# Latent attention projected feature-wise, its softmax weights and two other branches' scaled on ScalarE, and the first weight group converted in halves

## The reference, cut to what matters

```
u = rms_norm(h, norm_pre);  proj = u @ w_in
A: q  = rms_norm(c_q) @ w_uq        (192 -> 4 heads x (64 plain + 32 rotary))
   kv = rms_norm(c_kv) @ w_ukv      (128 -> 4 heads x (64 key + 64 value))
   rotary(q[64:96]), rotary(k_rope) shared by the heads; causal softmax(q k) v
B: dilated window attention;  C: top-128 keys of an indexer;  D: two softmax maps, p0 - lambda p1
y = concat(each branch * silu(gate)) @ w_out;  h = h + rms_norm(y, norm_post)
```

## Time and profile before

| | |
|---|---|
| median of three runs | 771.83 us (767.22 to 775.15) |
| the profiled execution | 768.9 us, its span 767.0 us |
| PE busy | 690.5 us, 90% of the span |
| DVE busy | 450.4 us, 59% |
| ACT busy | 328.7 us, 43% |
| POOL busy | 218.4 us, 28% |
| mean granted clock | 0.954 of full |

### The profile page before, as it was taken

The page is one execution under the profiler, slowest core; times in us unless marked ns, Lnnn a source line. Parts: engine busy times, 40 slices in busy tenths (PEclk is TensorE's granted clock), DMA queues, the critical chain, the costliest instruction groups (busy, mean ns, idle before and its releaser), DMA issues. The chain is left out here.

```text
span 767.0 us, 10353 instructions
## 1 busy us (share of the span) xinstructions
PE 690.5 (90%) x3836; PEld 553.9 (72%) x3836; DVE 450.4 (59%) x1067; ACT 328.7 (43%) x750; POOL 218.4 (28%) x91
## 2 busy tenths in 40 slices
PE   3996999998989899889998999999898989988996
PEld 2885877787776674448997887788787767444896
DVE  4211597987688645561182158888978864556214
ACT  4422534654223445571434345456432344457221
POOL 1332241424035430200335342324323543020020
PEclk9998999997899976999999999999999997699999
DMA  8457963423122110202353487542322221020112
GB/s 259 123 188 233 258 185 111 124 76 106 55 69 69 69 56 1 109 1 80 96 157 111 129 254 228 157 138 69 98 70 68 70 70 56 0 108 3 43 42 110
DMA packets 66753, 81.47 MB, mean 106 GB/s; under 512 B 10720, under 2 KB 52320, under 8 KB 66703
## 3 DMA queue, kind: packets, MB, share of 16 engines
q1 hardware_dynamic: 66703, 80.81, 34.2%
HBM read 70.28 MB, written 13.93 MB: 110 GB/s over the span
## 5 line engine op out<-in xcount | busy, mean ns | idle before, releaser
L694 POOL TENSOR_TENSOR w_low<-w_raw,w_high 128x2048 fp32r<-128x2048 f32 (+2 forms) x39 | 175.8, 4507 | 435.3 <-ACT w_high L733 435.3
L1215 PE MATMUL bank<-uT,w_high 128*128 128x512 f32 x400 | 161.2, 403 | 0.0
L1217 PE MATMUL bank<-uT,w_low 128*128 128x512 f32 x400 | 159.2, 398 | 0.0
L1216 PE MATMUL bank<-uT,w_high 128*128 128x512 f32 x400 | 159.1, 398 | 0.0
L837 ACT ACTIVATE probs<-probs,negmax 128x128 f32<-128x128 f32 (+3 forms) x160 | 89.1, 560 | 99.6 <-DVE negmax L1070 99.0
L1215 PEld LDWEIGHTS bank<-uT,w_high 128*128 128x128 f32 x400 | 76.2, 190 | 18.7 <-issue 1.9
L1217 PEld LDWEIGHTS bank<-uT,w_low 128*128 128x128 f32 x400 | 76.2, 190 | 18.0
L1216 PEld LDWEIGHTS bank<-uT,w_high 128*128 128x128 f32 x400 | 76.3, 191 | 16.5
L733 ACT ACTIVATE w_high<-w_raw 128x2048 fp32r<-128x2048 f32 (+2 forms) x40 | 74.7, 1868 | 29.8 <-DMA w_raw<-in_w_out 23.7
L1215 PE MATMUL bank<-w_high,mix 128*128 128x256 f32 x256 | 72.4, 283 | 1.0 <-DVE mix L1155 1.0
L1216 PE MATMUL bank<-w_low,mix 128*128 128x256 f32 x256 | 71.6, 280 | 0.0
(11 more groups left out here) (145 smaller groups left out, 1119.0 us busy)
## 6 DMA issues: line engine op xcount, KB each, us to landing
w_raw<-in_w_in SPq DMA_DIRECT2D x28, 1024.0 KB, 5.4
w_raw<-in_w_out SPq DMA_DIRECT2D x8, 1024.0 KB, 4.9
parts_dram<-staging SPq DMA_DIRECT2D x12, 512.0 KB, 5.9
strips<-strips_dram SPq DMA_DIRECT2D x24, 256.0 KB, 4.6
dqk<-parts_dram SPq DMA_DIRECT2D x24, 256.0 KB, 4.3
hX<-in_x SPq DMA_DIRECT2D x8, 512.0 KB, 5.8
strips_dram<-table_dram SPq DMA_DIRECT2D x1, 3328.0 KB
qidx<-parts_dram SPq DMA_DIRECT2D x12, 256.0 KB, 4.2
```

The costliest lines, as they stand in the source:

```text
L694: nc.gpsimd.tensor_tensor(w_low[:, s, :, 0:w], w_raw[:, s, :, 0:w], w_high[:, s, :, 0:w].bitcast(F32), ALU.subtract).then_inc(w_low_done, 1)
L1215: nc.tensor.matmul(out_ap, lh, rh, start=start, stop=False)
L1216: nc.tensor.matmul(out_ap, lh, rl, start=False, stop=False)
L1217: return nc.tensor.matmul(out_ap, ll, rh, start=False, stop=stop)
```

## The change

1. The order of the start is by token block: u0, cv0, u1, cv1, u2, cv2, u3, cv3, in both layers. In layer 0 group 0 is asked for before the second block of x, in two halves of its rows, and rounded (ACT) and reduced (DVE) in halves by a new step `first_low` behind u0. cv0 starts with the first half.
2. `norm` of the jobs of B, C and A: DVE takes only the reciprocal, ACT multiplies (four activations a job, 24 jobs in the two layers). D stays.
3. Branch A is projected feature-wise. `aq h`: one head's queries for all tokens, [128 x 512] in two products; the weight's columns are loaded so that rows 64 to 95 hold the rotary features and 96 to 127 the same with their halves swapped. ACT copies rows 0 to 63, and DVE multiplies rows 64 to 127 by cos and by -sin, sin (`trig`). The scores then contract over 128 rows. The query's root is not applied to q, but as a factor in the scores' L1070 (`negroot`). `aroot` spreads the key's root over the partitions by four products and DVE multiplies `latkv` by it; `ak`, `av` give keys (two heads each) and values.
4. The shared rotary key is made on POOL in three operations at `norm 8`, with two more loads, and copied by two transfers to the eight row groups of `aqk` at `norm 9`. `wuq` and `wukv` come in eight loads instead of three.

```diff
-HEAD_UNITS = [("u", 0), ("u", 1), ("unit", "cv", 0), ("u", 2), ("unit", "cv", 1), ("unit", "cv", 2), ("u", 3),
+HEAD_UNITS = [("u", 0), ("unit", "cv", 0), ("u", 1), ("unit", "cv", 1), ("u", 2), ("unit", "cv", 2), ("u", 3),
               ("unit", "cv", 3)]
...
+FIRST_START = [("hmean", 0), ("hnorm", 0), HEAD_UNITS[0], ("first_low",), ("hmean", 1), ("hnorm", 1), HEAD_UNITS[1],
+               HEAD_UNITS[2], ("hmean", 2), ("hnorm", 2), HEAD_UNITS[3], HEAD_UNITS[4], ("hmean", 3), ("hnorm", 3),
+               HEAD_UNITS[5], HEAD_UNITS[6], HEAD_UNITS[7]]
...
-    [HEAD_UNITS[1], 3, ("hmean", 3), HEAD_UNITS[2], HEAD_UNITS[3], ("hnorm", 3), HEAD_UNITS[4], HEAD_UNITS[5],
+    [HEAD_UNITS[1], HEAD_UNITS[2], 3, ("hmean", 3), HEAD_UNITS[3], HEAD_UNITS[4], ("hnorm", 3), HEAD_UNITS[5],
      HEAD_UNITS[6], HEAD_UNITS[7]]
...
-             10: [("aup", 0), ("aup", 1), ("aturn", 0)],
-             11: [("aup", 2), ("aturn", 1), ("aup", 3), ("aturn", 2), ("aturn", 3)]}
+             10: [("aq", 0), ("aq", 1), ("aroot",), ("aq", 2)],
+             11: [("aq", 3), ("ak", 0), ("ak", 1), ("av", 0), ("av", 1)]}
...
+                if step == ("norm", 8):
...
+                    nc.gpsimd.tensor_tensor(raw, raw, trig[HD:A_QK, :], ALU.mult).then_inc(kr_step, 1)
+                    pool.wait_ge(kr_step, 2 * l + 1)
+                    nc.gpsimd.tensor_tensor(turn, turn, trig2[HD:A_QK, :], ALU.mult).then_inc(kr_step, 1)
+                    pool.wait_ge(kr_step, 2 * (l + 1))
+                    nc.gpsimd.tensor_tensor(raw, raw, turn, ALU.add).then_inc(kr_ready, 1)
...
+                if kind == "first_low":
+                    w = WIDTH[0]
+                    for half in range(2):
+                        ks = slice(half * KC // 2, (half + 1) * KC // 2)
+                        act.wait_ge(first_loaded[half], 16 * len(GROUPS[0][1]))
+                        nc.scalar.activation(w_high[:, 0, ks, 0:w], w_raw[:, 0, ks, 0:w], ACT.Copy
+                                             ).then_inc(w_high_done if half else first_high, 1)
...
+                if kind == "norm" and MAPS[step[1]] == 1:
+                    j = step[1]
+                    buf = probs[probs_buffers(j)[0]]
+                    act.wait_ge(inv_ready, scaled(l, j))
+                    for q in range(NB):
+                        pr = buf[:, POFF[q]:POFF[q] + WID[q]]
+                        ins = nc.scalar.activation(pr, pr, ACT.Copy, scale=inv[:, j % 4, 0, q:q + 1])
+                    ins.then_inc(probs_scaled, 1)
...
+                if kind == "ak":
+                    n = l * NU + UNIT_AT[step]
+                    act.wait_ge(unit_ready, n + 1)
+                    for half in range(2):
+                        ins = nc.scalar.activation(aqk[0:HD, 1, 2 * step[1] + half, :],
+                                                   bank[HD * half:HD * (half + 1), unit_bank(n), :], ACT.Copy)
+                    ins.then_inc(emptied_by["act"], 1)
...
-                    after(nc.vector.reciprocal(inv[:, i, 0], sums[:, i, 0]))
-                    for q in range(NB):
-                        sl = slice(POFF[q], POFF[q] + WID[q])
-                        ins = nc.vector.tensor_scalar(probs[bufs[0]][:, sl], probs[bufs[0]][:, sl],
-                                                      inv[:, i, 0, q:q + 1], None, ALU.mult)
-                ins.then_inc(probs_ready, 1)
+                    nc.vector.reciprocal(inv[:, i, 0], sums[:, i, 0]).then_inc(inv_ready, 1)
...
+                if kind == "aq":
...
+                    dve.wait_ge(high_written, highs(n))
+                    nc.vector.tensor_tensor(aqk[HD:P, 0, step[1], :], bank[HD:P, unit_bank(n), :], trig[HD:P, :],
+                                            ALU.mult).then_inc(emptied_by["dve"], 1)
...
+                if kind == "aq":
+                    h = step[1]
+                    pe.wait_ge(a_folded, l + 1)
+                    b = work_bank(l * NU + UNIT_AT[step])
+                    nc.tensor.matmul(b, wuq[:, 0, h, :], latq[:, 0, :], start=True, stop=False)
+                    nc.tensor.matmul(b, wuq[0:QL - P, 1, h, :], latq[0:QL - P, 1, :], start=False, stop=True
+                                     ).then_inc(unit_ready, 1)
+                if kind == "aroot":
...
+                    for tb in range(NB):
+                        ins = nc.tensor.matmul(b[:, tb * P:(tb + 1) * P],
+                                               roots[:, r, NB + tb:NB + tb + 1].to_broadcast([P, P]), ident[:],
+                                               start=True, stop=True)
+                    ins.then_inc(unit_ready, 1)
+                if kind == "ak":
+                    wait_unit_emptied(pe, l * NU + UNIT_AT[("aroot",)])
+                    b = work_bank(l * NU + UNIT_AT[step])
+                    nc.tensor.matmul(b, wukv[:, 0, step[1] * P:(step[1] + 1) * P], latkv[:], start=True, stop=True
+                                     ).then_inc(unit_ready, 1)
```

More of the change, by code:

```diff
@@ L74 @@
 SEL_BLOCKS = (3, 2, 1)
-N_CONSTS = 12
+N_CONSTS = 10
 TOPK_ROUNDS = 3 * TOPK // 8
@@ L241, in units_of @@
         return ["dve"]
[L242 to L247, removed]
+    if k in ("aup_head", "aq", "aroot"):
+        return ["dve"]
+    if k in ("ak", "av"):
+        return ["act"]
     return []
@@ L338, in convert_steps @@
         for s in STEPS[freed + 1:]:
-            cost += {"unit": 1 if s[0] == "unit" and GROUPS[GI[s[1]]][2] else 2, "aup": 1, "pv": 1}.get(s[0], 0)
+            cost += {"unit": 1 if s[0] == "unit" and GROUPS[GI[s[1]]][2] else 2, "aq": 1, "ak": 1, "pv": 1}.get(s[0], 0)
             if cost >= CONVERT_AFTER.get(g, 4):
@@ L877, in _ @@
-                if kind == "aturn":
-                    tb = step[1]
-                    n = l * NU + UNIT_AT[step]
-                    for i in range(2):
-                        act.wait_ge(unit_ready, n + 1 + i)
-                        nc.scalar.activation(aqk[0:A_QK, i, :, tb * P:(tb + 1) * P],
-                                             bank[0:A_QK, unit_bank(n + i), :].rearrange(
-                                                 "p (h t) -> p h t", h=HEADS),
-                                             ACT.Copy).then_inc(emptied_by["act"], 1)
+                    act.wait_ge(unit_ready, n + 1)
@@ new lines, in _ @@
+                    nc.scalar.activation(aqk[0:HD, 0, step[1], :], bank[0:HD, unit_bank(n), :], ACT.Copy
+                                         ).then_inc(high_written, 1)
+                if kind == "ak":
+                    n = l * NU + UNIT_AT[step]
+                    act.wait_ge(unit_ready, n + 1)
+                    for half in range(2):
+                        ins = nc.scalar.activation(aqk[0:HD, 1, 2 * step[1] + half, :],
+                                                   bank[HD * half:HD * (half + 1), unit_bank(n), :], ACT.Copy)
+                    ins.then_inc(emptied_by["act"], 1)
@@ L886, in _ @@
+                if kind == "av":
+                    i = step[1]
+                    n = l * NU + UNIT_AT[step]
+                    if i == 0:
+                        act.wait_ge(pv_ready, l * NPV + PV_OF[7] + 1)
+                    act.wait_ge(unit_ready, n + 1)
+                    nc.scalar.activation(values[0][:, 2 * i:2 * i + 2, :].rearrange("p t c -> p (t c)"),
+                                         bank[:, unit_bank(n), :], ACT.Copy).then_inc(emptied_by["act"], 1)
                 if kind == "mix":
@@ L1399, in _ @@
+                if kind == "av":
+                    b = work_bank(l * NU + UNIT_AT[step])
+                    for half in range(2):
+                        tb = 2 * step[1] + half
+                        ins = nc.tensor.matmul(b[:, half * 256:(half + 1) * 256], latkv[:, tb * P:(tb + 1) * P],
+                                               wukv[:, 1, :], start=True, stop=True)
+                    ins.then_inc(unit_ready, 1)
                 if kind == "ya":
```

217 lines of the change are left out of this document (107 added, 110 removed).

## The result

The changed kernel takes 797.95 us (median of four runs, 793.57 to 805.73). The kernel before takes 772.5 on the same chip. The ratio is 1.0319 [1.0221, 1.0417]: slower, by about 25 us, where I had said 781 and a range up to 794. The direction was right, the size was not. The profiled executions differ by more than the medians, 799.7 against 767.0 us of span.

A forecast was written before the change was run, and what follows sets the result against it. PE, busy for 90% of the span, was taken as the bound. Terms 4.2 + 5.8 + 3.4 + 3.4 - 5.6 + 6.0 - 5.8 = +11.4 on 768.9 gave 780.3, stated as 781, range 766 to 794.

The forecast's parts named there:

- Clocks are set even: Whole kernel: half-clock time unchanged, what `turn 7` gets back against what new waits lose; nothing in the sum.
- The projections of A: From `aup_head` to the first A score, 40.0 before: feature-wise projections save 2.9 a layer, -5.8 in all.
- ScalarE's normalisation: ACT's multiplications delay awaited copies: +3.4 at bv, +3.4 at `pv 4`, -5.6 at `turn 7`, +6.0 in A's jobs.
- The jobs of A: Branch A's four jobs: ACT's multiplications don't fit beside its other work without delay, +3.0 a layer.
- The starts: Layer starts: cv units wait behind their own u and group 1's conversion, +4.2 in layer 0, +5.8 in layer 1.
- Further falls of the clock: Rival: new stretches without products at cv2 and bv lower the clock; three falls give 790, range 785 to 796, chance 0.20.
- The rival in which `turn 7` keeps the clock: 6.8 at half clock there goes, -3.4 a layer; with cheaper starts 767, one of both 774; shared chance 0.20.
- hiding ScalarE's work wholly: Rival: ACT's normalisation delays only where ACT was waited for; wholly hidden, 9 less, 772; chance 0.08.

The follow-up runs named there:

- e3: Feature-wise projections alone, in the kernel before (multiplications on DVE, old start): ratio 0.9911 [0.9851, 0.9971].
- e4: The changed kernel with the multiplications back on DVE, new start and projections kept: ratio 0.9998 [0.9932, 1.0064] to the kernel before.
- e9: e3 with job 7's weights multiplied by ScalarE, all else as in the kernel before: ratio 0.9899 [0.9834, 0.9964] to the kernel before.
- e1: ScalarE's multiplications alone, in the kernel before (old start, old projections): ratio 1.0223 [1.009, 1.0355].
- e5: The changed kernel with the old start, keeping ScalarE's multiplications and feature-wise projections: ratio 1.0286 [1.0231, 1.0342] to the kernel before.
- e12: The changed kernel with the dense products of e10 among the sums of squares: four executions, 801.16, 804.61, 798.17 and 776.41, too far apart for a ratio.
- e10: e9 with three dense products, results unread, among the sums of each token block: ratio 0.9847 [0.9749, 0.9945] to the kernel before.
- e6: The changed kernel with additional products, results unused, in PE's waits at cv2 of layer 0, bv2, `pv 4`, `pv 6`: ratio 1.0298 [1.0229, 1.0368] to the kernel before.
- e2: The new start alone (order by token block in both layers, group 0 early in halves), in the kernel before: ratio 1.0103 [0.998, 1.0227].
- e8: e3 with branch A's sums of squares one job slot earlier and job 7 multiplied by ScalarE: ratio 0.9931 [0.9886, 0.9975] to the kernel before.
- e7: The kernel before with branch A's sums of squares at the end of job slot 8 instead of 9: ratio 1.0381 [1.0301, 1.0461].

## Why the prediction was wrong

**The step that failed: the clock.** The sum has it in one sentence: "Clocks are set even: what `turn 7` gets back against what new waits lose." In the projections it keeps the stretch at half clock for a constant 17, as both layers of before showed it, and in branch A's jobs it has none. The traces, by stage, both layers together; the last column is the measured change less the forecast in the table above:

| stages | us at 1.2 GHz before | after | over the forecast |
|---|---|---|---|
| the two starts | 0 | 10.2 | +1.7 |
| cq to bv2 | 20.5 | 21.7 | -1.0 |
| bv2 to sums | 13.6 | 15.8 | +2.4 |
| sums to first A score | 34.2 | 51.2 | +10.9 |
| from the first A score on | 0 | 13.6 | +6.8 |
| sum | 68.3 | 112.5 | +20.8 |

The 44.2 us more at half clock are at most 22.1 of the 32.2 by which the two executions differ. The rest, 10.1 or more, stands against my 11.4: the waits were sized nearly right, and the clock, put at nothing, is the miss.

**The projections of A.** Forecast -5.8, in the changed kernel +5.1. The feature-wise code has 6.8 us at half clock or 24 to 27 (20.5 with the wait at `pv 6` filled), with stages of 31.9 or 41 (e3, e4). The long form comes with VectorE's multiplications too (four of six layers in e3, e4 and e9), so it isn't ScalarE's. In the changed kernel both layers were long: 27.3 and 23.9, that is 10.2 and 6.8 more than before, at most 8.5 of time. ACT's longer chain (4.5 for `pv 6` instead of 3.2) and the fold's 1.33 are the rest. That e3's ratio agrees with the -5.8 is luck in part: it rests on four of ten executions, and in e3's trace one layer gained 8.1 and the other lost 0.9.

**ScalarE's normalisation.** +7.2 forecast, 17 us alone (e1), and 16 to 25 within the whole (e4 against the changed kernel). Around bv2 the clock was nearly even, as set: `turn 7` gave back 6.8 us at half clock a layer, and the longer waits brought 6.8 in layer 0 and 10.2 in layer 1. With a wait of 3.00 the clock had held at bv2 in both layers of before; with 4.81 it fell in all eight layers that have it unfilled (e1, e5, e12 and the changed kernel). That isn't a rule: in e10 it fell beside bv2's 3.00 too, in both layers. e6 shows that the waits matter: filled, the stretches behind them go, and 4.9 us a layer come back in those two stages. The stretch behind `pv 6` (6.8 and 3.4) isn't ScalarE's alone, since e3, e4 and e9 have it behind a wait of 2.71.
The Trainium skill's "TensorE: Matmul & The Clock Gate" (section "HAM oscillation — how this bites in real kernels") says that a wait, there for a transfer, throttles the engine, so that the work behind it starts cold. Here the waits are for ACT's copies; the trace agrees by `pv 4`: a wait of 3.52, then 4.07 of work in a stretch at 0.50.

**The jobs of A.** +3.0 a layer forecast, +5.7 in layer 0. e1 has +2.3 at the full clock; the projections' other copies add 0.9 (e3); the rest, 2.4, is the 6.8 us at half clock, at most 3.4 of time. Here the parts meet: e1 has no half clock in these jobs, e3, e4 and e9 3.4 in one of two layers, e5 and the changed kernel 6.8 in every layer. The sum had nothing either for the 0.9 behind the jobs.

**The starts: right.** +4.2 and +5.8 forecast, +5.4 and +6.3 measured, and 8 to 11 for both alone (e2). POOL's remainder ahead of the root and `hnorm 3` behind it came as described. Most of what is over is cv2 of layer 0 at half clock.

**Against the rivals.** "Further falls of the clock" had 0.20 and 785 to 796; it was the case, and its count of three falls was too low. The rival in which `turn 7` keeps the clock was right in its part, and outweighed. Two sums are off: 780.3 and half of 2.9 are 781.8, not 781, and hiding ScalarE's work wholly would take away 3.4 + 3.4 + 6.0 = 12.8, not 9.

**What stays open.** What decides between the short and the long stretch in the projections. Of the twelve such stages with feature-wise projections, the sums in their old place and nothing added among them (e3, e4, e5, e6, e9 and the changed kernel, two layers each), two were short; with dense products among the sums, two of four. That may be chance, and the traces of e3, e4 and e5 are of executions longer than their medians, so the share of long ones needn't hold for all executions. With the sums a job slot earlier and dense units behind them, the feature-wise projections had 3.4 in both layers (e8), at the price of the stretch that began in the wait of 3.15. Whether the sums with one column, or the transposes and 64-row products just ahead of them, bring the clock down in the old place, no run isolates.

**Versions faster than both kernels by their ratios:** e3, e8, e9 and e10, with 0.9911, 0.9931, 0.9899 and 0.9847, all with intervals below 1. Their intervals overlap, and the gains are 2% or less. The medians of all executions bear out e8 (766.66 against 770.28), e9 and e10 (763.53 and 762.11 against 773.09), but not e3. Each has the feature-wise projections and neither the new start nor the multiplications on ScalarE, but for job 7's in the last three, at the one place where POOL had held DVE up.

## What to carry to other kernels

Where PE is the bound, a longer wait can cost twice: the wait, and the work behind it at half clock. Give each lengthened wait a stretch behind it in the sum, at up to half of what such stretches last in the trace. A stretch that stands in the old trace is no constant of the new code: 17 became 6.8 or 27. Where it decides the sign, give both as cases, and profile both layers and more than one execution before believing a gain of 1%. Work belongs on another engine where its own is held up at that moment (job 7: 6.76 to 1.92), not throughout; in a list that is worked in order, 1.9 ahead of an awaited copy is 1.8 of PE's time.

## What the runs showed of the hardware that was not expected

- The clock's state varies between layers and executions of the same code: the projections took 31.9 or 40.9 us in one execution (e3), 44.6 or 34.4 in another (e12). Runs of e3 lie between 761.59 and 780.88.
- fp32 products back to back don't always bring the clock back: in the changed kernel four pairs of `latq,wuq`, from 288.86 on, took 2.07 us each for 8 us and stayed at half clock. In e8 such pairs took 1.03 to 1.12.
- The clock can fall within a wait and stay down long after it: in e7 it fell at 296.7, in a wait of 3.98, and stood at half for 20.5 us, though PE was busy for 18.53 of the 21 from 297 on.
- DVE's update of a block of h took 5.80 us beside POOL's 4.75 when the two began together (e1), and 1.29 when it began 0.32 ahead of POOL (before).
- ScalarE's multiplication by a factor for each partition took 1.90 to 1.92 for 1280 columns in four pieces, from SBUF to SBUF; the copy of as many columns out of PSUM 1.68, VectorE's multiplication 1.27.
